# Output projection of a hybrid decoder layer: a third tile's weights split one stage earlier, and the first three tiles' weights in another order

## The reference, cut to what matters

```
h = RMSNorm(x)
proj = h @ w_in
o_dn  = gated DeltaNet, 6 heads       -> 6 x 128 columns
o_dil = dilated attention, 4 heads    -> 4 x 128 columns
o_nsa = sparse attention, 6 heads     -> 6 x 128 columns
x = x + concat(o_dn, o_dil, o_nsa) @ w_out        # the output projection
h = RMSNorm(x)
u = causal_conv3(h @ ffn_up); x = x + (silu(u_gate) * u_val) @ ffn_down
out = RMSNorm(x)
```

## Time and profile before

| what | us |
|---|---|
| median of 3 runs (2678.4 to 2680.92) | 2679.09 |
| the profiled execution | 2678.24 |
| its span in the trace | 2676.4 |
| PE busy in it | 2560.1 |
| DVE busy | 1404.3 |
| ACT busy | 855.4 |

### The profile page before, as it was taken

The page is one execution under the profiler, slowest core; times in us unless marked ns, Lnnn a source line. Parts: engine busy times, 40 slices in busy tenths (PEclk is TensorE's granted clock), DMA queues, the critical chain, the costliest instruction groups (busy, mean ns, idle before and its releaser), DMA issues.

```text
span 2676.4 us, 33433 instructions
## 1 busy us (share of the span) xinstructions
PE 2560.1 (96%) x11880; PEld 2089.7 (78%) x11880; DVE 1404.3 (52%) x2319; ACT 855.4 (32%) x1578; POOL 58.6 (2%) x42
## 2 busy tenths in 40 slices
PE   7999999989999998999999999999999999999996
PEld 4777777767788656888888888888888888888884
DVE  4776667734344565336444454545444444444446
ACT  4433323323224443224223232322323232323232
POOL 0111011100000000000000000000000000000000
PEclk9999999999999989999999999999999999999998
DMA  4311111121325022223222222222232222222222
GB/s 161 142 49 51 67 52 65 36 100 70 112 95 224 34 100 111 95 79 118 95 105 94 94 94 94 94 94 107 83 108 94 97 104 98 94 94 94 94 94 79
DMA packets 41593, 251.78 MB, mean 94 GB/s; under 512 B 5392, under 2 KB 5648, under 8 KB 13884
## 3 DMA queue, kind: packets, MB, share of 16 engines
q1 hardware_dynamic: 41532, 250.96, 26.1%
HBM read 243.04 MB, written 13.15 MB: 96 GB/s over the span
## 4 chain that ended last, share of the span: by engine, by line
PE 53%; DVE 1%; ACT 0%; issue 0%; DVEq 0%; ACTq 0%
PE bank L231 36%; PE bank L1670 18%; DVE x_t L1819 0%; DVE head_out L1750 0%; ACT head_out L1793 0%; DVE rms_row L1816 0%; PE bank L1772 0%; DVE x_t L1742 0%; PE bank L1657 0%; ACT rms_row L1795 0%; DVEq L1632 0%; ACTq L1792 0%; DVEq L1799 0%
## 5 line engine op out<-in xcount | busy, mean ns | idle before, releaser
L231 PE MATMUL bank<-h_hi,w_hi 128*128 128x512 f32 x2176 | 885.3, 407 | 35.0 <-DVE w_lo L191 30.5
L231 PE MATMUL bank<-h_lo,w_hi 128*128 128x512 f32 x2176 | 854.0, 392 | 0.0
L231 PE MATMUL bank<-h_hi,w_lo 128*128 128x512 f32 x2176 | 852.8, 392 | 0.0
L231 PEld LDWEIGHTS bank<-h_hi,w_hi 128*128 128x128 f32 x2176 | 412.3, 189 | 128.4 <-issue 18.3
L231 PEld LDWEIGHTS bank<-h_lo,w_hi 128*128 128x128 f32 x2176 | 410.9, 189 | 88.0
L231 PEld LDWEIGHTS bank<-h_hi,w_lo 128*128 128x128 f32 x2176 | 412.0, 189 | 84.4 <-issue 4.8
L182 ACT ACTIVATE w_hi<-w_raw_far 128x512 fp32r<-128x512 f32 x528 | 307.1, 624 | 439.5 <-PE bank L1670 274.8
L191 DVE TENSOR_TENSOR w_lo<-w_raw_far,w_hi 128x512 fp32r<-128x512 f32 x528 | 331.2, 686 | 123.9 <-ACT w_hi L182 122.6
L191 DVE TENSOR_TENSOR w_lo<-w_raw,w_hi 128x512 fp32r<-128x512 f32 x312 | 223.7, 757 | 193.1 <-ACT w_hi L182 192.9
L1670 PE MATMUL bank<-h_hi,w_hi 128*128 128x512 f32 x704 | 274.7, 390 | 1.0 <-DVE x_t L1742 1.0
L1670 PE MATMUL bank<-h_lo,w_hi 128*128 128x512 f32 x704 | 274.2, 390 | 0.0
(11 more groups left out here) (283 smaller groups left out, 1973.8 us busy)
## 6 DMA issues: line engine op xcount, KB each, us to landing
w_raw_far<-in_weights SPq DMA_DIRECT2D x132, 1024.0 KB, 4.8
w_raw<-in_weights SPq DMA_DIRECT2D x77, 1024.0 KB, 4.8
x_t<-in_x_t SPq DMA_DIRECT2D x7, 1024.0 KB, 9.8
bias_rows<-bias_row SPq DMA_DIRECT2D x10, 512.0 KB, 7.3
out<-x_t SPq DMA_DIRECT2D x8, 512.0 KB, 2.7
mix_scratch<-head_out SPq DMA_DIRECT2D x14, 256.0 KB
nsa_tab<-bias_rows SPq DMA_DIRECT2D x6, 448.0 KB, 7.4
h_lo<-mix_scratch SPq DMA_DIRECT2D x1, 2560.0 KB, 12.0
```

The lines of the kernel that those rows point to most:

```text
L231: m = nc.tensor.matmul(PB[pb][:], a[:, s, k], b, start=(kt == 0 and n == 0), stop=(kt == KT - 1 and n == 2))
```

## The change

The order of the quarters of output tiles 0, 1 and 2 is now a table: first quarters 0 to 2 of tiles 0 and 1, then quarters 0 to 2 of tile 2, and then the last quarter of each of the three. The units in DRAM are packed in that order. The attention step still does the first 24 steps. The projection's block does 24 steps for tiles 0 to 2 (before, 8 for tiles 0 and 1), of which the first 12 need no late head. Four more quarters are split at the end of the attention step, and one more unit is loaded in it. In the block the splits go one tile further ahead, x is waited for at `residual(0)`, and the norm weights at their first use.

```diff
+WO_QUARTERS = ((0, 0), (1, 0), (0, 1), (1, 1), (0, 2), (1, 2), (2, 0), (2, 1), (2, 2), (0, 3), (1, 3), (2, 3))
...
-        WO_PAIR = [(u, kt) for q in range(4) for u in range(2) for kt in range(4 * q, 4 * q + 4)]
+        WO_FRONT = [(u, kt) for u, q in WO_QUARTERS for kt in range(4 * q, 4 * q + 4)]
...
-            WO_EARLY = WO_PAIR[:3 * len(WO_PAIR) // 4]
+            WO_EARLY = WO_FRONT[:24]
...
             def nsa_act(act, r, last):
-                left = [4 if last else 8]
+                left = [8]
...
             def nsa_dve(dve, r, last):
-                left = [4 if last else 8]
+                left = [8]
...
                             load_mix(sp, range(a, a + NSA_R - 1), m_in[1])
+                        load_unit(sp)
                         load_unit(sp)
...
         def residual(dve, d):
-            dve.wait_ge(q_used, Q5 + (4 * (d + 1) if d else 7))
+            dve.wait_ge(q_used, Q5 + (4 * (d + 1) if d > 1 else 10 + d))
...
-                for u, kt in WO_PAIR[len(WO_EARLY):]:
+                for u, kt in WO_FRONT[len(WO_EARLY):]:
                     pe.wait_ge(m_lo, len(MIX_EARLY) if kt < MIX_LATE[0] else KT)
                     project(pe, u, kt)
-                for d in range(2, KT):
+                for d in range(3, KT):
...
-                act.wait_ge(g2_in, 32)
                 for d in range(KT):
-                    split_hi(act, 4 if d else 0)
+                    split_hi(act, 4 if d not in (1, KT - 1) else 0)
...
+                act.wait_ge(g2_in, 32)
                 act.wait_ge(lo_done, 4 * FFN_UNIT)
...
-                dve.wait_ge(xr_in, 64)
-                dve.wait_ge(g2_in, 32)
                 for d in range(KT):
-                    split_lo(dve, 4 if d else 0)
+                    split_lo(dve, 4 if d not in (1, KT - 1) else 0)
+                    if d == 0:
+                        dve.wait_ge(xr_in, 64)
                     if d < KT - 1:
                         residual(dve, d)
                         add_square(dve, d)
+                dve.wait_ge(g2_in, 32)
...
-    pair = [u.reshape(P, 4, QW) for u in units[-KT:-KT + 2]]
-    for i in range(2):
-        units[i - KT] = np.stack([pair[u][:, 2 * i + q] for q in range(2) for u in range(2)], axis=1).reshape(P, -1)
+    front = [u.reshape(P, 4, QW) for u in units[-KT:-KT + 3]]
+    for i in range(3):
+        units[i - KT] = np.stack([front[u][:, q] for u, q in WO_QUARTERS[4 * i:4 * i + 4]], axis=1).reshape(P, -1)
```

## The result

The changed kernel takes 2665.24 us (median of 5 runs, 2663.76 to 2668.57), the kernel before 2679.09 (2678.15 to 2680.92). The ratio is 0.995 (95% interval 0.9939 to 0.9961), so 13.8 us are saved. The forecast was 2666.3 in a range of 2664.3 to 2670.0. In a second comparison the changed kernel took 2665.34 and the one before 2678.63, a ratio of 0.9946 (0.9932 to 0.996).

A forecast was written before the change was run, and what follows sets the result against it. PE was taken to bound the kernel; 1.73 us (start), 8.14 (wait) and 2.51 (slow matmuls) made 12.4 saved. That gave 2665.8 from the profiled execution and 2666.7 from the median, so 2666.3, range 2664.3 to 2670.0.

The forecast's parts named there:

- What bounds: Whole kernel: PE, busy 2560.1 of 2676.4 us, sets the end; any gain at the seam goes straight through.
- Splits of unit 2 ahead of the barrier: End of attention: four low splits on DVE delay the second copy and the barrier; cost 0.3 us, between 0 and 2.5.
- PE starts at the barrier: Projection start: the first 12 steps need no late head, so PE starts earlier and saves 1.73 us.
- No wait for unit 2: Start of tile 2: quarters split before the barrier let the 72 matmuls run through; the wait's 8.14 us are saved.
- The clock: Behind the old wait: 12 matmuls no longer run at the lower clock, saving 2.51 us if the clock holds.
- the first rule: At the seam: idle TensorE drops to half clock until a spell of activity; under it the gain stays 12.4 us.
- The loss at the seam: At the barrier: transposes not counting as busy could lose the clock, costing 2.5 us; clock rival's chance 8%.
- Unit 3, x and unit 4: Projection block: earlier loads and splits and later waits cost nothing; unit 3 complete 9.6 us before PE needs it.
- The rival on x: Projection: x in only at 1067.4, 14 us later, stops PE; gain left some 4 us, 2675 us; chance 4%.
- the ring rival: Later projection tiles: last-quarter splits come late, PE stops at 13 tiles and loses 17 us, 2683.6 us; chance 3%.
- The total: Start of tile 3 and kernel end: 12.4 us saved; a gain of 11.5 to 12.8 us was given 80%.

The follow-up runs named there:

- before_again: The kernel before, unchanged, traced once more: seam up to the feed-forward part 174.80 us, against 174.61 in its first trace.
- e2: The kernel before with 32 unused matmuls put where PE stands idle for 8.0 us: seam 173.53 us, against 174.61 without them.
- e8: The kernel before with only unit 2's splits moved ahead of the wait for x: 2668.92 us against 2680.08, ratio 0.9958; seam 166.64 us.
- before: First trace of the kernel before, nothing changed: seam up to the feed-forward part 174.61 us.
- e1: The changed kernel with the last quarters of tiles 0 and 1 directly behind the barrier again: seam 163.91 us, against 162.01.
- e7: The kernel before with 14 unused matmuls at the start of the 8.0 us wait: seam 174.80 us, against 174.61 without them.
- changed: First trace of the changed kernel, nothing else altered: seam 162.01 us; this profiled execution took 2668.57 us.
- again: The changed kernel, unaltered, traced and timed once more: seam 162.07 us, median 2665.34 us.

## Why the prediction was right

*What bounds.* Right. The seam gained 12.6 us, and all of it went through to the end (1465.0 us from the second mark on in both).

*Splits of unit 2 ahead of the barrier.* The mechanism was described rightly, and its cost was too high: 0.3 us predicted, 0.01 measured (from the start of the last attention matmuls to the first transfer of x it is 3.54 us, and was 3.53). The low splits ran from 1038.84 to 1041.34, ended 0.54 us before the last attention matmuls, and left room for the first copy. The second copy began as directly behind these matmuls as before, where the prediction had it 0.1 to 0.4 us later. I had worked out that they end 0.33 us before PE, so 0.2 of the 0.3 us lies there, and the rest is that instructions which follow each other overlap by some 0.1 us.

*PE starts at the barrier.* The start term was 1.73 us. PE's idle time fell from 3.25 to 1.41 us, 1.84. Putting the order back costs 1.9. This term and the matmuls from the barrier to tile 3 (16.40 us, predicted 16.51) are each 0.1 us better than predicted, which makes the 12.6 out of the 12.4.

*No wait for unit 2.* The size was right, the reason given was not. The prediction had the splits ahead of the barrier as the cause. Splitting unit 2 behind the barrier gives the same seam (162.05), so it is in part luck that the size came out right. That PE can start at the barrier is due to the new order and packing, which have two quarters of tile 2 in unit 1. That it doesn't stop later is due to unit 2's split no longer standing behind `residual(0)`, and so behind x. Moving just that, in the kernel before, yields the larger part of the gain.

*The clock.* 2.5 us predicted for the 12 slow matmuls. The filled idle time gave back 5.25 - 2.8 = 2.45 us and shows the cause. As the first rule quoted from the Trainium skill has it ("TensorE: Matmul & The Clock Gate", Part 1), it is idle time that loses the clock. The loss at the seam that I drew from its Part 4 did not occur: the changed kernel's two traces have 1.00 there. But PE's work before the barrier is not full of transposes, as I wrote: of the 49 PE instructions in the row of 1028 to 1040 only 10 are (line 1219), so that row could not speak for or against a loss by transposes. One argument of the prediction was weak, though. It said that 3.25 us of idle time leave the clock alone. In six traces with this idle time at the barrier the clock fell in three (before_again, e2 and e8) and held in three (before, e1 and e7).

*Unit 3, x and unit 4.* Right in what they cost. Unit 3's last quarter was split at 1050.4, and PE came to unit 3 9.3 us later (predicted: 9.6). Its early load is worth 1.8 us, and waiting for x at its use is worth nothing. `residual(0)` came at 1056.74, 13.6 us behind the first transfer of x, where the prediction had 12.8, and PE never waited for it. In all five traces of the changed code in which `residual(0)` waits for x alone it is 13.6 to 13.8 us. Why x takes longer there than in most traces of the code before stays open. The rival on x was priced wrong: with x in at 1067.4 PE would only begin to stop, and for a gain of 4 us x would have to come some 8 us later still. In the rest of the projection PE has no wait, so the ring rival is out too.

*The total.* 12.4 predicted against the own time, 12.6 measured at the seam, and 13.8 and 13.3 in the medians. The medians' gains lie above the 11.5 to 12.8 us that I gave 80%, though the time is within the range. The difference of about 1 us to the medians isn't settled. x is on the path of the kernel before, and in the three other traces where it is on the path it took 12.8, 13.0 and 14.2 us, which would make the kernel before somewhat slower on average than its profiled execution. That a longer x goes through to the seam is shown (e7: 0.20 us more of x, 0.19 of seam), how much it is on average is not. A scatter ahead of the seam is shown: its first mark lies between 980.07 and 985.99 us in twelve traces, and the step behind it takes either 56.1 to 56.7 or 58.1 to 58.2 us, whichever kernel it is. The three long ones (changed, again and e2) have a clock of 0.66 in the stretch from 19 to 29 us behind the first mark, and the nine short ones have 0.83 there. So the long step goes with a longer time at the lower clock. For e2 this stretch is about 1000 to 1010 us:

```profile
1000.00:1010.00 10.00, 8.77 (x26) 5.40 (x27) 7.32 (x19) 5.19 (x14) 0.00 (x0) 0.66 0.08 34
```

(e2, whose code up to there is that of before.)

## What to carry to other kernels

Where the busiest engine stands still, look at what stands ahead of the awaited instruction in its own engine's program, not only at what it needs: here four splits needed nothing but a weight unit that had long arrived, and stood behind an addition that needed 4 MB. Moving them alone saved 8.0 of the 12.6 us. And price a wait on TensorE with the slow matmuls that follow it: 8 us of idle time cost 10.6.

When a part of a change is costed, ask which data the first instruction really needs. I credited the early split of unit 2 with a gain that is there without it, since two of tile 2's quarters lie in unit 1 and the rest can be split behind the barrier, ahead of the wait for x.

## What the runs showed of the hardware

- An idle time of TensorE of 3.25 us lost the full clock in three of six traces. The idle times of 5.0, 5.4 and 8.0 us, one trace each, lost it. Those of 1.41 and 1.45 us kept it in all five traces that have them. After a loss, matmuls of 128 x 512 start 0.43 us apart instead of 0.23: 12 or 13 of them in five of the six losses, which costs 2.5 to 2.7 us, and 8 in the sixth (e2, at the barrier), which costs 1.7.
- The same 4 MB of x took between 12.8 and 14.2 us from the first issue to the first use in five traces in which the loads around it stand as before, and 13.6 to 13.8 us in five of the changed kernel and its variants.
- With the same code for PE, the last attention step up to its last matmuls took 58.1 to 58.2 us in three traces, which have a granted clock of 0.66 in the stretch from 19 to 29 us into it, and 56.1 to 56.7 us in the nine that have 0.83 there.
- The time up to a given instruction differs by up to 5.9 us from run to run at 980 us into the kernel. A gain of 1 us can be read in a trace from two marks around it, where five timed runs don't show it.
